# The opening of a fused two-block transformer kernel: modulation weighed by two engines, and three units begun together

## The reference

```python
mod = c @ w_ada[l] + b_ada[l]                      # c: 1 x 1024, w_ada: 1024 x 3072
shift, scale, gate = jnp.split(mod, 3, axis=-1)
h = rmsnorm(x, pre_norm_g[l]) * (1.0 + scale[:, None, :]) + shift[:, None, :]
proj = h @ w_in[l]                                 # 1024 x 11264
q, k, v, z_ret, u_val, u_gate, z_conv, g_a, g_b = jnp.split(proj, split_at, axis=-1)
```

## Time and profile before

| what | value |
|---|---|
| median of 3 runs | 1729.02 us (1728.03 to 3334.2) |
| the profiled execution's own time | 1730.86 us |
| its span, first to last instruction | 1729.0 us |
| busy: PE, PEld, DVE, ACT, POOL | 94%, 71%, 64%, 51%, 37% |
| mean granted clock of PE | 0.976 |
| chain that ended last, by engine | PE 61%, DMA 17%, DVE 12%, issue 6%, ACT 3% |
| DMA | 340.98 MB, 197 GB/s on average |

### The profile page before, as it was taken

How to read it: one execution, slowest core, us unless ns; L and a number is a source line. 1 busy time by engine, 2 the same in 40 slices (tenths; PEclk the granted TensorE clock), 3 DMA queues, 4 the chain that set the end, 5 groups by cost and what they waited for, 6 DMA issues and landing times.

```text
span 1729.0 us, 22131 instructions
## 1 busy us (share of the span) xinstructions
PE 1625.4 (94%) x7116; PEld 1220.4 (71%) x7116; DVE 1100.1 (64%) x1449; ACT 879.8 (51%) x1241; POOL 631.2 (37%) x373
## 2 busy tenths in 40 slices
PE   3899999999999999999989998995999999999996
PEld 3788888777878788778878887683666665665654
DVE  6776865371422448433576543336999999999986
ACT  4544533433222333234455334433877877877775
POOL 0578886333324335324464433110122222222221
PEclk9999999999999999999998999996999999999998
DMA  9343444143121153532223221256999999999993
GB/s 324 103 116 111 138 151 160 55 146 103 50 104 49 49 219 134 195 122 93 98 69 109 74 98 49 56 204 251 379 403 405 398 407 400 398 388 377 391 389 123
DMA packets 135424, 340.98 MB, mean 197 GB/s; under 512 B 14596, under 2 KB 66060, under 8 KB 110521
## 3 DMA queue, kind: packets, MB, share of 16 engines
q1 hardware_dynamic: 127938, 320.71, 49.8%
q0 software_dynamic: 5200, 8.41, 2.2%
q10 hardware_dynamic: 2215, 10.93, 1.6%
HBM read 329.78 MB, written 18.87 MB: 202 GB/s over the span
## 4 chain that ended last, share of the span: by engine, by line
PE 61%; DMA 17%; DVE 12%; issue 6%; ACT 3%; DVEq 1%; SPq 0%; POOLq 0%; ACTq 0%; POOL 0%
PE ps L768 17%; PE ps L769 17%; PE ps L770 17%; DMA ring<-in_w 16%; PE ps L740 5%; DVE parts L2388 3%; PE ps L750 2%; DVE act_parts L2388 2%; PE ps L1128 1%; DVE arena L2431 1%; PE ps L1015 1%; DMA ring<-in_w_ada 1%; DVE arena L2447 1%; DVE arena L2081 1%; ACT parts L1226 1%
## 5 line engine op out<-in xcount | busy, mean ns | idle before, releaser
L2502 POOL TENSOR_TENSOR parts<-ring,parts 128x1024 fp32r<-128x1024 f32 x172 | 426.0, 2482 | 620.2 <-ACT parts L1226 617.0
L1226 ACT CAST parts<-ring 128x1024 fp32r<-128x1024 f32 x174 | 180.5, 1048 | 363.3 <-PE ps L770 327.7
L768 PE MATMUL ps<-parts,act_parts 128*128 128x512 f32 (+2 forms) x832 | 327.4, 394 | 7.5 <-DVEq L1909 3.0
L769 PE MATMUL ps<-parts,act_parts 128*128 128x512 f32 (+2 forms) x832 | 322.5, 388 | 0.0
L770 PE MATMUL ps<-parts,act_parts 128*128 128x512 f32 (+2 forms) x832 | 322.4, 387 | 0.0
L768 PE MATMUL ps<-act_parts,parts 128*128 128x512 f32 x640 | 252.0, 394 | 5.0 <-DVEq L1814 5.0
L769 PE MATMUL ps<-act_parts,parts 128*128 128x512 f32 x640 | 249.7, 390 | 0.0
L770 PE MATMUL ps<-act_parts,parts 128*128 128x512 f32 x640 | 249.5, 390 | 0.0
L768 PEld LDWEIGHTS ps<-parts,act_parts 128*128 128x128 f32 (+1 forms) x832 | 150.4, 181 | 72.8 <-issue 32.5
L1601 ACT CAST parts<-ring 128x1024 fp32r<-128x1024 f32 x144 | 144.7, 1048 | 75.7 <-PE ps L770 70.2
L770 PEld LDWEIGHTS ps<-parts,act_parts 128*128 128x128 f32 (+1 forms) x832 | 150.3, 181 | 39.3
(11 more groups left out here) (295 smaller groups left out, 2502.8 us busy)
## 6 DMA issues: line engine op xcount, KB each, us to landing
arena<-in_w SPq DMA_DIRECT2D x96, 1024.0 KB, 13.2
ring<-in_w SPq DMA_DIRECT2D x96, 1024.0 KB, 14.8
ring<-in_w_in SPq DMA_DIRECT2D x30, 1024.0 KB, 7.3
ring<-in_w_in SPq DMA_DIRECT2D x34, 512.0 KB, 5.2
ring<-in_w_ada SPq DMA_DIRECT2D x12, 1024.0 KB, 10.4
ring<-in_w_ret_out SPq DMA_DIRECT2D x8, 1024.0 KB, 6.3
ring<-in_w_out SPq DMA_DIRECT2D x8, 1024.0 KB, 7.6
ring<-in_w_in SPq DMA_DIRECT2D x16, 256.0 KB, 4.1
```

The lines of the kernel that those rows point to most:

```text
L768: pe.matmul(o, lhs[1], rhs[0], start=start, stop=False)
L769: pe.matmul(o, lhs[0], rhs[1], start=False, stop=False)
L1226: act.copy(parts[:, g % 4, 0, :], ring[:, st.place(j), k * 1024:(k + 1) * 1024]).then_inc(dense_hi, 1)
L2502: pool.tensor_tensor(parts[:, g % 4, 1, :], ring[:, st.place(j), k * 1024:(k + 1) * 1024], parts[:, g % 4, 0, :].bitcast(F32), ALU.subtrac ...
```

## The change

It does these things:

- SP: each ada chunk's first half raises a semaphore of its own (`ada_half_landed`), the second half raises `weights_landed`, to which DVE adds the first half's 16 by a nop.
- DVE: `weigh_rows` takes rows t = 0 to 5 of an ada chunk (`ADA_ROWS = 6`), the first four as soon as the first half has landed. It no longer releases the ada chunks. It takes the modulation out of PSUM ahead of subtracting a piece, with two more small additions, and subtracts one piece instead of two.
- PE: for each ada chunk it forms the rows t = 6 and 7 itself, straight from `ring` with a column of c (8 products a chunk, into columns 16 and up of the bank), then the sums of DVE as before. It releases the ada chunks. The order is chunk 0, chunk 1, four tiles of transposes, chunk 2, four tiles, chunk 3. The "mod" bank comes ahead of "hT" in the plan.
- PE in the conv stage begins three units together: units 0 and 1 on tiles 0 and 1, unit 2 on tiles 0 and 1, then all three on tiles 2 to 7.
- ACT rounds the third piece between tiles 1 and 2 of `actT`.
- POOL subtracts from the second piece on, instead of the third.
- Three semaphores that nobody waits for are gone, with the nops that raised one of them.

```diff
-    ("columns", 1, 1), ("hT", KT, 1), ("mod", (1,), 1), ("conv", [CONV_BANKS[(k + 1) % 6] for k in range(5 * KT)], 1), ("hq0", GROUP_A, 1),
+    ("columns", 1, 1), ("mod", (1,), 1), ("hT", (0, 2, 3, 4, 5, 6, 7, 0), 1), ("conv", [CONV_BANKS[(k + 1) % 6] for k in range(5 * KT)], 1), ("hq0", GROUP_A, 1),
+ADA_ROWS = 6
...
+            def ada_halves(j):
+                st = chunks["ada"]
+                s, n = st.place(j), st.before(j)
+                if n:
+                    sp.wait_ge(weights_used[s], n)
+                (dst, src), rest = pair(ring[:, s, :], w_ada[:, :, j * 512:(j + 1) * 512])
+                sp.dma_start(dst, src).then_inc(ada_half_landed[j % 2], 16)
+                sp.dma_start(*rest).then_inc(weights_landed[s], 16)
...
-            pe.wait_ge(h0_ready, MT)
-            for t in range(KT):
-                turn("hT", t, [h0[:, m, t * P:(t + 1) * P] for m in range(MT)])
-
-            o = bank("mod", 0)
-            for g in range(4):
+            mod = bank("mod", 0)
+
+            def mod_columns(g):
+                place = chunks["ada"].place(g)
+                w = landed("ada", g).rearrange("p (k n) -> p k n", k=KT)
+                for c in range(4):
+                    for t in range(ADA_ROWS, KT):
+                        mm = pe.matmul(mod[:, 16 + 4 * g + c:17 + 4 * g + c], w[:, t, c * P:(c + 1) * P], c_col[:, t:t + 1],
+                                       start=t == ADA_ROWS, stop=t == KT - 1)
                 pe.wait_ge(ada_ready, g + 1)
                 n = 2 if g < 3 else 1
                 for c in range(4):
-                    mm = product(o[:, 4 * g + c:4 * g + c + 1], [ada_sum[:, 2 * g + q, c * P:(c + 1) * P] for q in range(n)],
+                    mm = product(mod[:, 4 * g + c:4 * g + c + 1], [ada_sum[:, 2 * g + q, c * P:(c + 1) * P] for q in range(n)],
                                  [cst("ones")[:, 0:1]] * n)
-            filled("mod", 0, mm)
+                    if c == 0:
+                        mm.then_inc(weights_used[place], 1)
+                return mm
+
+            mod_columns(0)
+            mod_columns(1)
+            pe.wait_ge(h0_ready, MT)
+            for t in range(KT):
+                if t == KT // 2:
+                    mod_columns(2)
+                turn("hT", t, [h0[:, m, t * P:(t + 1) * P] for m in range(MT)])
+            filled("mod", 0, mod_columns(3))
...
-            first = [(bank("conv", n), conv_weights(n)) for n in range(2)]
-            for t in range(KT):
-                pe.wait_ge(actT_ready, t + 1)
-                for n, (o, w) in enumerate(first):
-                    mm = conv_step(o, w, t)
-                    if t == KT - 1:
-                        filled("conv", n, mm)
-            for n in range(2, 5 * KT):
+            first = [bank("conv", n) for n in range(3)]
+            for ts, units in (((0, 1), (0, 1)), ((0, 1), (2,)), (range(2, KT), (0, 1, 2))):
+                for t in ts:
+                    pe.wait_ge(actT_ready, t + 1)
+                    for n in units:
+                        mm = conv_step(first[n], conv_weights(n), t)
+                        if t == KT - 1:
+                            filled("conv", n, mm)
+            for n in range(3, 5 * KT):
...
             for t in range(KT):
+                if t == 2:
+                    ahead(3)
                 act.activation(actT[:, 0, t, :], x0T[:, t, :], ACT.Identity, bias=mod_shift[:, t:t + 1],
...
-                dve.wait_ge(weights_landed[s], (st.before(j) + 1) * 32)
+                rows = ADA_ROWS if stage == "ada" else KT
+                if stage == "ada":
+                    dve.wait_ge(ada_half_landed[j % 2], (j // 2 + 1) * 16)
+                    dve.nop().then_inc(weights_landed[s], 16)
                 w = ring[:, s, :].rearrange("p (k n) -> p k n", k=KT)
-                for t in range(KT):
+                for t in range(rows):
+                    if t == (KT // 2 if stage == "ada" else 0):
+                        dve.wait_ge(weights_landed[s], (st.before(j) + 1) * 32)
...
-                dve.nop().then_inc(weights_used[s], 1)
+                if stage == "gate":
+                    dve.nop().then_inc(weights_used[s], 1)
...
-            for g in range(2):
-                stage, j, k, last = PIECE_CHUNK[g]
-                s = chunks[stage].place(j)
-                dve.wait_ge(dense_hi, g + 1)
-                dve.tensor_tensor(parts[:, g, 1, :], ring[:, s, k * 1024:(k + 1) * 1024],
-                                  parts[:, g, 0, :].bitcast(F32), ALU.subtract).then_inc(dense_split, 1)
-            dve.wait_ge(dense_split, 2)
-            dve.nop().then_inc(weights_used[s], 1)
             o = full("mod", 0)
             own(dve.tensor_tensor(mod_shift, o[:, 0:KT], cols[:, :, ROWS - 2], ALU.add))
             own(dve.tensor_tensor(mod_scale, o[:, KT:2 * KT], cols[:, :, ROWS - 1], ALU.add))
             own.wait()
+            own(dve.tensor_tensor(mod_shift, o[:, 16:16 + KT], mod_shift, ALU.add))
+            own(dve.tensor_tensor(mod_scale, o[:, 16 + KT:16 + 2 * KT], mod_scale, ALU.add))
+            own.wait()
...
             dve.nop().then_inc(mod_ready, 1)
+            dve.wait_ge(dense_hi, 1)
+            dve.tensor_tensor(parts[:, 0, 1, :], ring[:, chunks["conv"].place(0), 0:1024], parts[:, 0, 0, :].bitcast(F32),
+                              ALU.subtract).then_inc(dense_split, 1)
...
-            split_to = [2]
+            split_to = [1]
...
-            pool.wait_ge(dense_split, 2)
+            pool.wait_ge(dense_split, 1)
```

More of the change, by code:

```diff
@@ L446, in build @@
             "gates_stored", "gates_in", "gates_used", "merged_ready"))
-        ms_ready, rms_ready, x_ready = (sem(n) for n in ("ms_ready", "rms_ready", "x_ready"))
+        ms_ready, rms_ready = (sem(n) for n in ("ms_ready", "rms_ready"))
         x_rms_ready, in2_r_ready = sem("x_rms_ready"), sem("in2_r_ready")
@@ L475, in build @@
         conv_stored, conv_back = sem("conv_stored"), sem("conv_back")
-        block_w_ready, slot_w_ready, idx_out_ready = sem("block_w_ready"), sem("slot_w_ready"), sem("idx_out_ready")
+        block_w_ready, idx_out_ready = sem("block_w_ready"), sem("idx_out_ready")
         settled = sem("settled")
+        ada_half_landed = [sem(f"ada_half{n}_landed") for n in range(2)]
         out_done = sem("out_done")
@@ L555, in ada @@
                 chunk(stage, j, lambda r: pair(r, w_ada[:, :, g * 512:(g + 1) * 512]))
+            def ada_halves(j):
[6 more added lines that the diff above has]
+                sp.dma_start(*rest).then_inc(weights_landed[s], 16)
             sp.wait_ge(const_in, 16)
-            ada("ada", 0, 0)
+            ada_halves(0)
             sp.wait_ge(x_in, 16)
-            ada("ada", 1, 1)
+            ada_halves(1)
             sp.wait_ge(weights_landed[0], 32)
-            ada("ada", 2, 2)
+            ada_halves(2)
             sp.wait_ge(weights_landed[1], 32)
-            ada("ada", 3, 3)
+            ada_halves(3)
             for t in range(KT):
@@ L2016, in _ @@
                 dve.tensor_tensor(x[:, m, :], x[:, m, :] if m else x0_early, y_tok[:, m, :], ALU.add).then_inc(row_ready, 1)
-            dve.nop().then_inc(x_ready, 1)
             low_T("h2T", 6, TAPS + 3)
```

## The result

The changed kernel took 1734.3 us (median of 11 runs, 1730.81 to 1740.69), the kernel before 1729.6 us beside it (median of 11). The ratio is 1.0037, with a 95% interval of 1.0022 to 1.0052: 3.8 to 9.0 us slower, within 2%. The ratio leaves out the one run of the kernel before that took 3334.2 us; by it the two lie 6.4 us apart, by the medians 4.7. The forecast was 1736.5 us, +7.5 on the kernel before. The profiled execution took 1736.47 us, its span is 1734.5.

A forecast was written before the change was run, and what follows sets the result against it. PE, 94% busy, was taken to bound the kernel. At half clock +7.3 (modulation) and +2.5 (tiles) give +9.8; possible clock rises make it +7.5, so 1729.0 + 7.5 = 1736.5 us, range 1728.0 to 1740.5.

The forecast's parts named there:

- The forecast's case: Opening: PE becomes the later engine, unbroken from 19 to about 50; 1736.5 us, own range 1733.5 to 1739.5, chance 0.6.
- A: Start of the first actT tile on ACT, 45.25 before; forecast about 52.5 at half clock throughout, +7.3 us.
- 16 can go either way: Opening: each burst of 16 transposes on PE may or may not raise its clock; even or slightly lower chance each.
- The savings: Opening: a clock rise after the first transpose burst saves about 3.4 us, after the second up to 2.4.
- rival (b): Opening: both transpose bursts raise PE's clock and the tiles go smoothly; +1 to +4 us, 1730 to 1733, chance 0.17.
- A + 25.6: Conv stage's start: third unit's end, against A + 23.05 before; +2.5 us, bounds -1 to +4.
- DVE is not the last there: Modulation before the change: DVE's last chunk ready about 41.7, PE ending 2.9 us later, already behind.
- The later release of the ring places: Opening: PE frees chunk 2's place near 40.5 instead of 35.34; w_in's delay stays hidden, 8 us to spare.
- half chunks: Modulation: with fewer rows, DVE's last sum comes 1.3 to 3.5 us earlier, helping only if PE is not later still.
- Rival (a): Opening: DVE's chain is the bound, PE keeps up at 0.11 us a record, A near 41; 1725 to 1727, chance 0.13.

The follow-up runs named there:

- e3: Changed kernel, but PE begins two conv units together as before the change, the third behind them; 1735.8 us, ratio 1.0030.
- e1: Changed kernel, but DVE weighs all eight rows of each ada chunk again and PE forms only the sums; 1731.4 us, ratio 1.0008.
- e2: Changed kernel, but ACT rounds the first two pieces between its copies, DVE subtracts both before taking the modulation, POOL begins with the third; 1731.6 us, ratio 1.0008.
- e6: Changed kernel, but DVE waits for the whole ada chunk before its first row, not for the half; 1732.8 us, one run.
- e4: Kernel before the change, but PE begins three conv units together and ACT rounds the third piece between tiles 1 and 2; 1729.8 us, ratio 1.0003.
- e7: Changed kernel, but PE does all 32 transposes in a row behind chunk 0, then chunks 1, 2, 3; 1735.7 us, one run.
- e9: Changed kernel, but DVE weighs seven rows, joins its sums for every chunk and subtracts both first pieces; 32 transposes behind chunk 1; 1724.4 us, ratio 0.9985.
- e10: As e9, but all 32 transposes come right behind chunk 0, ahead of chunk 1; 1726.1 us, ratio 0.9982 to the kernel before.
- e5: Changed kernel, but DVE joins its two sums for every ada chunk, not the last alone, 24 PE records fewer; 1731.0 us, ratio 1.0011.
- e8: Changed kernel, with eight idle 128x256 products added on PE ahead of chunk 0, into an unused bank; 1734.6 us, one run.

## Why the prediction was right or wrong

**Right: which engine is late.** The forecast's case said that PE becomes the later engine, without a gap from 19 to about 50. It is (the ten rows above), and DVE waits 8.70 us for it. The times of the groups were forecast at half clock as 26.0, 32.8 and 36.2, and measured 25.98, 32.81 and 36.25. With the clock at half throughout, A was to be 52.5; e3 is that case and measured 52.8. That the two rows are the cause is shown by e1 (A 43.0, 4.2 us earlier without them).

**Open before, and still: the clock.** "16 can go either way" is what the runs show. Both bursts raised it in the changed kernel's trace, e2 and e6 (A 47.1 to 47.2), whose PE stream in the opening is the same, neither in e3. The savings were sized at 3.4 and 2.4 us. Chunk 2's 32 records took 3.8 us (36.25 to 40.03) instead of 6.8, so 3.0; chunk 3's 24 took 2.9 (43.29 to 46.2) instead of 5.1, so 2.2. The traced execution is thus rival (b), and its opening, +2.9 at G, lies in that rival's +1 to +4. I had given either burst an even or slightly lower chance; three traces of four show both. Weighed so, three at +2.9 and one at +8.5 (e3's, 264.0 less the 1.3 of the third unit, against 254.2), the mean is +4.3. The medians say +4.7, the ratio +6.4. This is arithmetic on four traces, not a measured frequency, and can't tell how often the clock rises. That the profiled execution took 1736.47 us where 1736.5 was forecast is luck: of its distance to the profiled execution of before, only 2.9 us come from the opening and 2.2 from the expert stage, which the forecast had no term for.

**Over-sized: the tiles.** The term that came out wrong is "A + 25.6", +2.5 on before; the third unit ended at A + 24.0 (71.2 less 47.2), +1.0. All three POOL pieces struck one DVE operation each, as forecast (2.73, 2.38 and 2.46 us). Tile 1 was ready at A + 7.8 rather than A + 8.6, and PE's stretch at half clock cost 1.2 us rather than 2. The loop of three units brings 1.3 us (e3, e4), the late subtraction with its third POOL piece costs 2.7 (e2).

**Too strong: "DVE is not the last there".** In the traced execution of before PE was later, by 0.5 us. But e4 shows an execution in which DVE's subtraction of two pieces was the last, with the same A (in part because its last chunk landed 0.4 later). Before, the two engines were nearly level. The change shortened one and lengthened the other, so the time could only follow the longer. That holds with either reading, which is why the error cost nothing.

**Right: what was costed at nothing.** The later release of the ring places stayed hidden: ACT rounded the third and fourth pieces at 48.59 and 53.77 with no wait ahead of them. The half chunks buy next to nothing (e6).

**The clock and the transposes.** In the changed kernel's trace a 128x1 record costs 0.213 us ahead of a burst of transposes and 0.12 behind it, with nothing else between. The Trainium skill's rule that transposes don't count as busy for the clock ("TensorE: Matmul & The Clock Gate", Part 4: PE-mode transpose) doesn't fit that trace, nor those of e2, e6 and e7; in e3 the same bursts raised nothing, which the rule would allow.

**Rival (a)** ended where its condition wasn't met: 0.213 us a record up to 32.8 rather than 0.11. With few enough records on PE (e9), its opening at A 41 was reached, with a median of 1724.4.

## What to carry to other kernels

Before work is moved from a busy engine to another, lay both engines' lists beside each other in the stretch and see how far apart they end. Here they were 0.5 us apart, and 64 added records of 0.11 to 0.21 us could only lose. A product with one column costs PE its weight loads (two records of 0.11 or 0.21 us here), so sums over partitions belong on PE only after another engine has folded them down as far as it can for nothing. In e9 one burst of 32 transposes ahead of 32 small records kept all of these at full clock; with 88 behind the burst (e7) 56 of them ran at half. So a burst helps the small products right behind it only if these are few.

## What the runs showed of the hardware that was not expected

**The same instructions get a different clock in one trace and in another.** In the opening that is worth 5.3 us (A 47.2 or 52.8, less 0.3 for the later landing). Only one execution of each kernel was traced, and e3's program differs from the changed kernel's behind the opening. All ten timed runs of e3 have a mean granted clock of 0.980 to 0.986, where the changed kernel's eleven have 0.974 to 0.984, and the stretch ahead of the first recorded change counts as 1.00 in that mean. So the edit may have made the slow opening more frequent; no run settles that. A different clock is worth about 5 us once more, in the attention of the second block. PE's line of scores in the changed kernel and in e3 (ns min/median/max, first start to last start):

```profile
L979 PE MATMUL ps<-arena x64: 376/376/792, 870.1 to 938.1; 64*128 64x256 f32 x64
```
```profile
L978 PE MATMUL ps<-arena x64: 375/377/481, 876.5 to 939.7; 64*128 64x256 f32 x64
```

68.0 us against 63.2 for the same 64 matmuls; the longest is 792 ns in the one, 481 in the other. The windows of the same 70 us (busy of PE, PEld, DVE, ACT, POOL, then the granted clock):

```profile
860.00:930.00 70.00, 64.48 (x279) 51.02 (x278) 47.23 (x72) 38.09 (x82) 35.45 (x15) 0.88 0.17 61
```
```profile
860.00:930.00 70.00, 64.34 (x309) 52.22 (x308) 44.07 (x64) 37.08 (x73) 34.57 (x15) 0.95 0.22 75
```

The granted clock is 0.88 against 0.95 (0.95 too in e3's 866.4 to 936.4, which is the same work): PE stood at 1.2 GHz for part of the stretch in the first and for much less of it in the second. Four of the twelve traces (e3, e6, e9, e10) have the short form, and no edit touches this stage. So e3, 6.9 us late at G, ends with the same span of 1734.5 us as the changed kernel: 4.8 us of it come back here, the rest elsewhere. Whoever compares two single executions of this kernel compares mostly this. The runs of the kernel before, one program, show it in their totals: beside e5 to e8, the eight with a mean granted clock of 0.978 to 0.981 took 1724.9 to 1727.7 us, the five with 0.975 to 0.977 took 1728.7 to 1733.3. The changed kernel's runs don't sort so: its three at 0.979 took 1730.8 to 1740.7. The marks inside the trace separate an edit's effect from it; medians of some ten runs leave 2 to 3 us of uncertainty.
